# Sixteen-chunk projections of the last two layers with one 512-column matmul for both parts of the input, and VectorE adding the two halves of the bank

## The reference

```python
def even_layer(h, w_in, ...):                       # layer "b" of the kernel
    z = h @ w_in                                    # 2048 -> 1024+1024+1024+128+128+1024
    lru_x, lru_gate, q, k, v, swa_gate = split_cols(z, EVEN_SPLITS)
    lru_x = causal_depthwise_conv(lru_x, conv_w, conv_b)
    y_a = rg_lru(lru_x, ...) * jax.nn.silu(lru_gate)
    y_b = sliding_window_gqa_sinks(q, k, v, sinks) * jax.nn.silu(swa_gate)
    return jnp.concatenate([y_a, y_b], axis=-1) @ w_out

def odd_layer(h, w_in, ...):                        # layer "d"
    z = h @ w_in
    c_q, c_kv, k_rope, mla_gate, dq, dk, dv, diff_gate = split_cols(z, ODD_SPLITS)
    ...                                             # latent attention and differential attention
    return jnp.concatenate([y_c, y_d], axis=-1) @ w_out

for layer in range(2):
    x = x + (even_layer, odd_layer)[layer](rmsnorm_2(x, norm_gains[layer]), ...)
return rmsnorm_2(x, final_norm_gain)
```

## Time and profile before

| | us |
|---|---|
| median of 3 runs | 2292.22 |
| lowest, highest | 2289.57, 2292.61 |
| the profiled execution, its time | 2291.38 |
| the profiled execution, its span | 2289.6 |

### The profile page before, as it was taken

How to read it: one execution, slowest core, us unless ns; L and a number is a source line. 1 busy time by engine, 2 the same in 40 slices (tenths; PEclk the granted TensorE clock), 3 DMA queues, 4 the chain that set the end, 5 groups by cost and what they waited for, 6 DMA issues and landing times.

```text
span 2289.6 us, 38450 instructions
## 1 busy us (share of the span) xinstructions
PE 2060.2 (90%) x14546; PEld 1344.3 (59%) x14546; DVE 1250.8 (55%) x2275; ACT 867.9 (38%) x1329; POOL 45.8 (2%) x52
## 2 busy tenths in 40 slices
PE   5899999989988888888888888999999999999998
PEld 2677767762222222222222222799899999998898
DVE  3556567554444444444444444777766554468655
ACT  3343345432111111111111111667756544466654
POOL 0000000000000000000000000010100000011000
PEclk9999999999999999999999999999999999999999
DMA  9998887889999999999999999744445555553443
GB/s 367 383 350 317 310 288 278 304 331 411 427 428 428 427 428 428 427 427 428 427 427 428 428 427 427 256 148 148 138 148 186 174 178 183 183 157 116 142 126 114
DMA packets 121943, 695.42 MB, mean 304 GB/s; under 512 B 13536, under 2 KB 13664, under 8 KB 60384
## 3 DMA queue, kind: packets, MB, share of 16 engines
q1 hardware_dynamic: 121824, 693.78, 78.6%
HBM read 691.63 MB, written 2.10 MB: 303 GB/s over the span
## 4 chain that ended last, share of the span: by engine, by line
PE 45%; DMA 35%; DVE 10%; ACT 5%; issue 3%; SPq 3%; DVEq 0%; ACTq 0%
DMA ring<-in_w 30%; PE acc L1324 28%; DVE WL L2080 3%; DMA land<-in_stream_a 3%; PE acc L1321 3%; PE psO L1383 3%; PE psS L1592 3%; ACT WH L1761 2%; SPq L1136 2%; DMA land<-in_stream_bc 1%; PE psM L1190 1%; PE acc L1190 1%; DVE HL L2093 1%; PE psO L1263 1%; DVE X L2236 1%
## 5 line engine op out<-in xcount | busy, mean ns | idle before, releaser
L2080 DVE TENSOR_TENSOR WL<-land,WH 128x1024 fp32r<-128x1024 f32 (+2 forms) x350 | 421.8, 1206 | 384.2 <-ACT WH L1761 379.6
L1324 PE MATMUL acc<-HH,WH 128*128 128x256 f32 x2000 | 585.2, 293 | 7.8 <-DVE HL L2093 3.5
L1324 PE MATMUL acc<-HH,WL 128*128 128x256 f32 x2000 | 568.0, 284 | 0.0
L1324 PE MATMUL acc<-HL,WH 128*128 128x256 f32 x2000 | 567.7, 284 | 0.0
L1761 ACT ACTIVATE WH<-land 128x1024 fp32r<-128x1024 f32 (+2 forms) x350 | 362.5, 1037 | 203.1 <-PE acc L1324 147.7
L1324 PEld LDWEIGHTS acc<-HH,WH 128*128 128x128 f32 x2000 | 385.1, 193 | 31.2 <-issue 12.6
L1324 PEld LDWEIGHTS acc<-HH,WL 128*128 128x128 f32 x2000 | 385.5, 193 | 2.2 <-issue 1.7
L1324 PEld LDWEIGHTS acc<-HL,WH 128*128 128x128 f32 x2000 | 385.2, 193 | 0.0
L1592 PE MATMUL psS<-ring,low 128*32 128x512 f32 x2048 | 272.7, 604 | 101.8 <-DMA ring<-in_w 100.1
L1592 PEld LDWEIGHTS psS<-ring,low 128*32 128x32 f32 x2048 | 40.8, 108 | 311.9 <-DMA ring<-in_w 282.6
L1922 ACT ACT_TABLE_LOAD x32 | 41.1, 1283 | 441.9 <-PE psS L1592 441.9
(11 more groups left out here) (433 smaller groups left out, 2601.8 us busy)
## 6 DMA issues: line engine op xcount, KB each, us to landing
ring<-in_w SPq DMA_DIRECT2D x384, 1024.0 KB, 26.0
land<-in_stream_bc SPq DMA_DIRECT2D x246, 512.0 KB, 4.2
land<-in_stream_a SPq DMA_DIRECT2D x92, 1024.0 KB, 8.1
land<-in_stream_a SPq DMA_DIRECT2D x100, 512.0 KB, 6.8
land<-in_stream_bc SPq DMA_DIRECT2D x12, 384.0 KB, 3.7
X<-in_xT SPq DMA_DIRECT2D x1, 2048.0 KB, 15.5
out<-low SPq DMA_DIRECT2D x3, 512.0 KB, 2.7
cst<-in_const SPq DMA_DIRECT2D x1, 1514.5 KB, 10.9
```

What stands on the lines that cost most here:

```text
L1324: mm = pe.matmul(bank[:, 0:S], w[:, kk, :], h[rows[kk]], start=(z == 0 and i == 0), stop=stop)
L2080: ins = dve.tensor_tensor(wl, src, wh, ALU.subtract)
```

## The change

It concerns the projections with sixteen chunks of layers b and d, except `dv` (and those from latents, which have six or four chunks): the names in `FOLDED`, 77 projections, and `wb` and `wc`, 32.

- The high and the low part of the input lie at a fixed distance, so one matmul can read both: `mix_pair` gives 2x256 columns. A half is now eight matmuls of 512 columns with WH (both parts, one to each half of the bank) and then eight of 256 columns with WL (HH, into the first half of the bank). TensorE waits for `hi` before the first eight and for `lo` only before the second eight.
- The result is the sum of the bank's halves. For the 77 a new step `fold` on VectorE adds them into one of two 128x256 buffers `folded`. The step `evac` of that projection waits for it and reads the buffer instead of the bank; it stays on ScalarE (`bk`: on VectorE). The bank is free after `fold`.
- For `wb` and `wc` there is no copy on ScalarE and no `res`: VectorE adds first the one half and then the other to X. The squares, and for `wc` the multiplication with the final gain, are appended after the loaded half instead of before it.
- At the start of layer b the squares and sums for the norm are moved: six squares ahead of the projections, the rest around `bq` 1 and 2, and the norm's factor between the halves of `bq` 3.

The core of the diff:

```diff
+FOLDED = ("bq", "bk", "bv", "bs", "lx", "lg", "cq", "ckv", "kr", "dk", "dq", "dg", "mg")
 def evac_by(x):
-    return "dve" if x[0] in ("bk", "p") or x == LAST_OUT else "act"
+    return "dve" if x[0] in ("bk", "p", "wb", "wc") else "act"
...
             self.acc.append(("proj", x))
+        if x[0] in FOLDED:
+            self.folds.append(x)
+            self.add("dve", "fold", x)
         self.add(evac_by(x), "evac", x)
...
+                two_halves = name in ("wb", "wc") or name in FOLDED
+                if two_halves:
+                    needs(k, "act", o, "hi", q)
+                else:
+                    needs(k, o.lo_by[q], o, "lo", q)
...
+                if two_halves:
+                    for kk in order:
...
+                        pe.matmul(bank[:, :].rearrange("p (z s) -> p z s", z=2), wh[:, kk, :], mix_pair(k, name, rows[kk]),
+                                  start=(i == 0 and kk == order[0]), stop=False, skip_group_check=True)
+                    needs(k, o.lo_by[q], o, "lo", q)
+                    for kk in order:
+                        mm = pe.matmul(bank[:, 0:S], wl[:, kk, :], HH[rows[kk]], start=False,
+                                       stop=(last and kk == order[-1]), skip_group_check=True)
...
                     if n >= 2:
...
-                        needs(k, evac_by(x), o, "evac", x)
+                        if x[0] in FOLDED:
+                            needs(k, "dve", o, "fold", x)
+                        else:
+                            needs(k, evac_by(x), o, "evac", x)
...
                     a = bank[:, 0:S] if bank is not None else None
+                    if name in FOLDED:
+                        needs("dve", "fold", x)
+                        a = folded[:, o.folds.index(x) % 2, :]
...
-                        if name == "wc":
+                        if name in ("wb", "wc"):
+                            then(dve.tensor_tensor(X[:, n, :], X[:, n, :], bank[:, S:2 * S], ALU.add))
                             ins = dve.tensor_tensor(X[:, n, :], X[:, n, :], bank[:, 0:S], ALU.add)
...
+                    elif what == "fold":
+                        x = step[1]
+                        f = o.folds.index(x)
+                        needs("pe", "proj", x)
+                        if f >= 2:
+                            last = o.folds[f - 2]
+                            if evac_by(last) == "act":
+                                needs("act", "evac", last)
+                        bank = acc[o.acc.index(("proj", x)) % 2]
+                        ins = dve.tensor_reduce(folded[:, f % 2, :], bank[:, :].rearrange("p (z s) -> p s z", z=2), AX.X, ALU.add)
```

More of the change, by code:

```diff
@@ L271, in proj @@
         if post == "res":
-            if x != LAST_OUT:
+            if x[0] not in ("wb", "wc"):
                 self.add("dve", "res", x)
@@ L669, in order_bc, with norm_factor @@
             o.load()
+    for m in range(6):
+        o.add("act", "sqm", m)
     o.proj(("bq", 0), first=1)
+    for m in (1, 2):
+        o.add("dve", "sqsum", ("moe", m))
     o.proj(("bq", 1), first=1, loads=2)
-    for m in range(4):
+    for m in (6, 7):
         o.add("act", "sqm", m)
-        if m:
-            o.add("dve", "sqsum", ("moe", m))
+    for m in (3, 4, 5):
+        o.add("dve", "sqsum", ("moe", m))
     o.proj(("bq", 2))
-    for m in range(4, 8):
-        o.add("act", "sqm", m)
+    for m in (6, 7):
         o.add("dve", "sqsum", ("moe", m))
[L680 to L684, removed]
+    halfway = [False]
+    def norm_factor():
+        if not halfway[0]:
+            o.add("pe", "ssm")
+            o.add("dve", "ssum", "moe")
+            o.add("act", "sqrtn", "moe")
+            o.add("dve", "rstd", "moe")
+        halfway[0] = True
+    o.proj(("bq", 3), between=norm_factor)
     o.proj(("bk",))
@@ L894, in program @@
         sti = sb("sti", [P, 64], I32)
+        folded = sb("folded", [P, 2, S])
         arena_at = (nc.sbuf_base + 31) // 32 * 32
@@ L1309, in product @@
                 normed = {("p", 0): "x0", ("k", 0): "x", ("bq", 0): "moe", ("cq", 0): "wb"}.get(x)
+                if two_halves:
+                    for kk in order:
+                        if normed:
+                            needs(k, "dve", o, "hl", normed, rows[kk])
+                        if x in (("wb", 0), ("wc", 0)) and kk % 4 == 0:
+                            needs(k, "dve", o, "ml", name, rows[kk] // 4)
+                        pe.matmul(bank[:, :].rearrange("p (z s) -> p z s", z=2), wh[:, kk, :], mix_pair(k, name, rows[kk]),
[4 more added lines that the diff above has]
+                                       stop=(last and kk == order[-1]), skip_group_check=True)
+                    mm.then_inc(done[k]["pe"], 1)
+                    return
                 for tt in range(NT if wide else 1):
@@ L1315, in product @@
                             needs(k, "dve", o, "cl", *(("cq", kk) if name == "qr" else ("ckv", kk)))
-                        if x in (("wp", 0), ("wo", 0), ("wb", 0), ("wc", 0)) and term == 0 and kk % 4 == 0:
-                            needs(k, "dve", o, "ml", "wo" if name == "wp" else name, rows[kk] // 4)
+                        if x in (("wp", 0), ("wo", 0)) and term == 0 and kk % 4 == 0:
+                            needs(k, "dve", o, "ml", "wo", rows[kk] // 4)
                         stop = last and z == len(terms) - 1
@@ L1771, in run @@
                         else:
-                            needs("dve", "res", (name, 4 * (c // 8) + c % 4 if name == "moe" else c))
+                            needs("dve", *(("evac", (name, c)) if name == "wb" else ("res", (name, 4 * (c // 8) + c % 4))))
                             if name == "wb" and c == 0:
@@ L1833, in run @@
                         n = x[1]
-                        needs("dve", "evac" if x == LAST_OUT else "res", x)
+                        needs("dve", "evac" if x[0] in ("wb", "wc") else "res", x)
                         sq = W((aSQ if k == 0 else dSQ) + n % 2)[:, 0, :]
@@ L1845, in run @@
                         n = step[1]
-                        needs("dve", *(("evac", LAST_OUT) if n == KD - 1 else ("res", ("wc", n))))
+                        needs("dve", "evac", ("wc", n))
                         ins = act.activation(W(MIX + n)[:, 0, :], X[:, n, :], ACT.Copy, scale=C("gain_f", n, 1))
@@ L2287, in run @@
                             continue
+                        keys = folded[:, o.folds.index(x) % 2, :]
                         for g in range(2):
```

34 lines of the change are left out of this document (19 added, 15 removed).

## The result

The changed kernel takes 2384.76 us (median of 4 runs, 2380.53 to 2386.33), the kernel before 2292.41 in the same comparison (4 runs, 2289.57 to 2294.57). The ratio is 1.041, with a 95% interval from 1.0397 to 1.0423: 92 us more, where 78 were forecast. The span of the profiled execution is 2381.8 us.

What follows compares the result with a forecast made beforehand. TensorE was taken to bound these stages, VectorE following. VectorE's added fold and waiting, mostly in the attention stages (+50, +26), outweighed TensorE's savings: +78 us in sum, median 2370 us, 8-in-10 range 2314 to 2418.

Steps and rivals of the forecast that it cites:

- half of -8.5: `wb` and `wc`, no fold: 32 projections save 0.35 us each, less early waits; -8.5 us together (-11 to 0).
- The hand-off: After each fold VectorE stands still for ScalarE's copy and `hi`: 1.68 us, or 2.4 us a projection with the fold.
- How much of the old waits for `hi` stays: Attention stages: half of VectorE's earlier waits for `hi` kept, from 34.8 and 25.5 us, with none and all as ends.
- The rival in which they vanish: Both attention stages: all old waits for `hi` vanish (+32, +13); about +26 us in all, 2318; chance 0.13.
- The head: 1436 to 1482 us, 6 projections: VectorE needs 53 us against 46; +7 us (0 to +12), moved squares the same work.
- The fold: On VectorE, 512 elements read from PSUM: 692 ns by the nearest reduction, 0.72 us with the gap.
- The wide matmul: On TensorE, 512 columns taken as 0.218 us: a chunk saves 22 ns (0 to 27), all 109 projections 38 us.
- `dk` and `dq` at 5.4 us a projection: Sign expected in the changed kernel's profile, instead of 5.76 us, with the wait hidden and the saving kept (-5.5 us).
- `cq` and `ckv`: 1780 to 1855 us, 11 projections: just even, sums of squares on TensorE wait for a later evac; 0 (-4 to +5).
- The clock: TensorE's longer waits before `T` bring more spells at 1.2 GHz, of which a part costs; +4 us (0 to +15).
- The rival in which the lateness feeds on itself: Sixteen jobs: waits before `T` bring some 14 more spells at 1.2 GHz, 40 us on top, 2410; chance 0.10.
- TensorE the bound throughout: Rival for all stages: all 109 projections save in full, 38 us less, 2254, faster; chance 0.10.

Runs made afterwards that it cites:

- the wait alone: Kernel before, with ScalarE's evac of each of the 77 projections also waiting for the VectorE step ahead of the fold's place; 2353.85 us, ratio 1.0276.
- the work alone: Kernel before, with one VectorE reduction of 512 elements per projection at the fold's place, which nobody waits for; 2296.07 us, ratio 1.0021.
- the exchange on ScalarE: Changed kernel, with ScalarE's `hi` of the half loaded at a projection's end put ahead of that projection's evac; 2322.31 us, ratio 1.0139 to the kernel before.

## Why the prediction was right

The ends of TensorE's last matmul of each stage, in both traces, give the terms one by one, in us:

| stage | forecast | measured |
|---|---|---|
| first layer, to the first product of `bq` 0 | 0 | -3.9 |
| head, to the last `bv` | +7 | +9.4 |
| first attention stage, to the last `lg` | +50 | +53.6 |
| `wb` | half of -8.5 | +1.4 |
| `cq`, `ckv`, `kr` | 0 (-4 to +5) | +6.4 |
| `dk`, `dq` | -5.5 | -2.7 |
| `dv` | 0 | 0.0 |
| second attention stage, to the last `mg` | +26 | +23.2 |
| to the last `vm` | +5 | +7.8 |
| `wc` | half of -8.5 | -3.7 |
| behind the last `wc` | 0 | +0.8 |
| sum | +78, with +4 for the clock | +92.2 |

The first row is no effect of the change: nothing is edited in the first layer, and in the eleven profiles of this case the first product of `bq` 0 starts anywhere from 1435.4 to 1441.3 us.

- *The hand-off.* Added up as 1.68 us; the trace has 1.73, in 68 of the 77 cases within 0.3 of it. It is the copy from `folded`, 0.42 us, that is longer than the one from PSUM, 0.38. That the coupling and not the work decides was argued then; the wait alone (63 us), the work alone (5 us) and the exchange on ScalarE (62 us back) show it.
- *How much of the old waits for `hi` stays.* The middle was taken for want of a view that splits them. The changed kernel's trace splits them. In the first attention stage VectorE waits 65.4 us for `hi`, 48.9 of them directly behind the 28 folds, so 16.5 of the old kind are left where 17.4 were forecast; in the second it is 42.5, of which 25.7 stand behind folds, so 16.8 where 12.8 were forecast. The rival in which they vanish falls.
- *The head.* The total is within the stated 0 to +12. But only 6.5 of the 9.4 us go with the fold (51.9 us from the first product to the last `bv`, 45.3 in the kernel without fold); 2.9 stay without it. The prediction took the moved squares as the same work at no price. TensorE's one long wait there is for the sum of these squares on VectorE; it took 1.5 us in the kernel before and takes 8.1 here:

```profile
PE psM L1513 <- DVE high_bc L2286: 8.1, 1, 8.1
```

- *The fold*, 0.691 against 0.692 us of the earlier trace rows.
- *The wide matmul.* This term was mis-sized: 0.218 us was taken, from plain float32, and 0.230 measured. The saving of a chunk is 10 ns and not 22. The narrow matmul's 256 columns are 0.107 us at 2.4 GHz and it costs 0.120, so 13 ns come on top; 512 columns are 0.213, and 17 ns come on top. The overhead of a matmul of this type did not shrink with its size, and the earlier trace rows were the wrong neighbour. The rule of the Trainium skill (TensorE: Matmul & The Clock Gate, "Back-to-back issue gap"), 216 ns, lay 14 ns under the row here, as it lay 11 under the narrow one. The term was -14 us for the 48 projections of `wb`, `wc`, `dk` and `dq` and came out at -5.1; 48 x 16 x 10 ns = 7.7 would be all of it. Of the signs to look for, `dk` and `dq` at 5.4 us a projection did not come: their ends lie 5.59 us apart. `wb` even got longer: TensorE waits 2.9 us in it where it waited 2.4, and runs a spell at 1.2 GHz behind that, where before there was none.
- *`cq` and `ckv`.* Forecast even, with the sums of squares named and priced at 5 us at most; 6.4 measured, and the row for it (6.8 us in two waits) is the same in the kernel that folds only outside the attention stages.
- *The clock.* Forecast: more spells at the lower level. They came, in the first attention stage a mean of 0.90 instead of 0.98. The price was to be small as long as VectorE sets the pace, and filling TensorE's waits won nothing in either attention stage. What the +4 us were for does not show as a row of its own. The rival in which the lateness feeds on itself, 2410, is not borne out.
- *TensorE the bound throughout*, 2254: out by the same rows that put VectorE's free time at 1.5 us and the demand at 2.4. The changed kernel has TensorE busy for 207 of 255 us in the first attention stage. The weight loads, by which (beside the share of peak arithmetic) the Trainium skill (Perfetto Trace Analysis, "Identifying the Most-Contended Engine") would judge, did fall, from 185 us in 202 to 171 in 255; less of them bought no time here. Without the fold the bound is TensorE's indeed, but the gain is 13 us and not 38.

The sum was 14 us short: 9 in `wb`, `wc`, `dk` and `dq`, 6.4 in `cq`, `ckv` and `kr`. The rest cancels: 9.6 us more than forecast at the head, in the first attention stage, up to `vm` and behind `wc`, against 10.7 less in the second attention stage, for the clock and in the first layer. That they cancel is luck; that the two attention stages come within 4 us each, from the hand-off as it was added up, is not.

## What to carry to other kernels

When a step moves from one engine to another, ask not only how busy the new engine is but what stands behind the step on the old one. Here VectorE had room for 53 us of work, at a price of 5; letting ScalarE wait for it cost 63, because ScalarE's next instruction feeds VectorE. Two in-order queues that wait for each other once per turn run as one; put the work that the other engine needs ahead of the wait (62 us here), or keep the new wait to stages where both have time to spare (`dk` and `dq`: 2.7 us gained there, 8 with `wb` and `wc`, which have no fold). And work that is nearly free outside such a ring is not free inside it: the same 53 us cost 5 without the wait and 35 with it.

## What the runs showed of the hardware

- A matmul of 128x128 weights of the `F32R` type follows the last after 0.230 us with 512 columns and 0.120 with 256, each 13 to 17 ns over its columns at 2.4 GHz. Joining two into one saves 10 ns, 4%.
- Filling TensorE's waits with matmuls of ones brought the mean granted clock of a stage from 0.92 to 1.00 and did not change its time (131.4 us): in that stage, where TensorE waits for the others, its lower clock cost nothing.
- A copy of 128x256 on ScalarE takes 0.38 us from PSUM and 0.42 from SBUF.
